# A decoder layer on one core: the gating unit between the last slabs of the input projection, and the first half of the output projection slab by slab between the heads of the attention

## The chip, the core and the metric

The kernel runs on one core of a Trainium2 chip. TensorE (PE) multiplies into PSUM, eight banks of 128 x 512 fp32; VectorE (DVE), ScalarE (ACT) and GpSimd (POOL) compute; SyncE (SP) starts most of the transfers between HBM and SBUF, POOL the others. The metric is the device time of one execution in microseconds (us). The median of three runs is 1489.71 us (1485.79 to 1490.67).

## The reference, cut to what matters

```python
mod = jnp.dot(jax.nn.silu(c), p['w_ada']) + p['b_ada']
shift1, scale1, gate1, shift2, scale2, gate2 = jnp.split(mod[:, None, :], 6, axis=-1)
h = x * (1 + scale1) + shift1
proj = jnp.dot(h, p['w_in'])
q, k, v, u_a, v_a = jnp.split(proj, [W_B, 2 * W_B, 3 * W_B, 3 * W_B + W_A], axis=-1)
...
attn = moba_attention(q, k_all, v_all, pos0, p['rel_bias'])
u_a = jax.nn.gelu(u_a)
v_a = layer_norm(jax.nn.gelu(v_a), p['ln_sgu_g'], p['ln_sgu_b'])
gm = chunk_spatial_gate(u_a, v_a, p['w_s'], p['b_s'])      # u_a * (w_s @ v_a + b_s)
mixed = jnp.concatenate([rms_norm(gm, p['norm_a_g']), rms_norm(attn, p['norm_b_g'])], axis=-1)
x = layer_norm(ALPHA * x + gate1 * jnp.dot(mixed, p['w_out']), p['ln1_g'], p['ln1_b'])
h = x * (1 + scale2) + shift2
up = jnp.dot(h, p['w_up'])                                  # then conv, silu, w_down, layer norm
```

There are 288 rows: 256 of one prompt and 32 of eight sampled sequences (four tokens each, with 256 old keys and values in pages of 128). The model width is 2048, with eight gating groups and eight attention heads of 128 columns. Everything is fp32.

## The kernel before

All activations lie transposed: a tile is 128 features by 288 rows. Each engine has one instruction stream, written out by hand, and semaphores join the streams; their order in the code is the order on the engine.

A weight matrix is read in **slabs** of 128 x 1024 fp32 (0.5 MB). ACT rounds a slab to fp32r (`hi`, tile wH), DVE subtracts to get the rest (`lo`, tile wL), and PE makes three products for each 128 x 128 block (L401 to L403), so 24 matmuls of 288 columns a slab (`products`). Four slabs are in flight (`RING`), three split ahead (`AHEAD`). ACT's `hi` for slab i+3 waits until slab i-1 is used. PE's `take` waits until the last reader of a PSUM bank has released it.

The **input projection** has 80 slabs: five chunks of the model width, ten groups of four output tiles in each; the last chunk is slabs 60 to 79, two for each group, and DVE adds each finished tile to `proj`. Between slabs stand **bursts** of four modulation slabs (`ada_slab`, w_ada, 0.5 MB each, ring of 8): 128 of the 192 modulation slabs are done there. When a unit of 16 is through, ACT copies it, PE turns it (`ada_turn`) and DVE adds it to modT (`mod_finish`).

After slab 79 comes everything that needs `proj`: transposes of v and of the gating unit's v_a, statistics, scaling, gate matmuls (wsT and bd), u times gate; then the attention in a loop over eight heads: scores of head h+1, the scores of one sampled sequence's old keys (`past_scores`, KV), one modulation slab, then softmax, transpose (`Pp` to `PTp`) and product with `Vrm`. Sixteen modulation slabs stand in the gating unit, eight between the heads, eight later. The **first half of the output projection** (slabs `S_OUT` to `S_OUT`+15, tiles 0 to 7 of the mixed rows, which come from the gating unit) starts after the last head, with the old values' products of the sampled sequences between the slabs; the **second half** (16 slabs, the attention's rows) follows, then a layer norm whose chain is DVE and ACT work (`normalise`, `centre`, `affine`), and the up projection.

KV is a double buffer of 1 MB halves; POOL refills a half (`load_kv`, two pages, two transfers) when the step that read it is through (`kv_used`).

Of the kernel before, what the change touches and what calls it, by code (L numbers as in the profile page):

```python
# [53 lines left out]
OUT_BANKS = (2, 3, 6, 7)  # L54
# [8 lines left out]
CHUNKS = [(0, 2), (2, 2), (4, 4), (8, 4), (12, 4)]  # L63
IN_SLABS = [(c, g, half) for c, (_, nk) in enumerate(CHUNKS) for g in range(IN_GROUPS) for half in range(nk // 2)]
# [9 lines left out]
def slab_columns(s):  # L74
# [7 lines left out]
TD_UP = [TD_OUT + 3 * n for n in (8, 20, 32)]  # L82
TD_DN = [TD_OUT + 3 * 16, TD_OUT + 3 * 28, TD_OUT + 3 * 37 + 1]
# [5 lines left out]
A_GATE, A_UP = 128, 160  # L89
# [19 lines left out]
def ada_turn_of(a):  # L109

    return a // ADA_RING if a < A_GATE else A_GATE // ADA_RING + (a - A_GATE) // RING


UNIT_END = {q: min(i for i in range(-1, IN_N) if ada_through(i) >= a + n) for q, (a, n, _, _) in enumerate(MOD_UNITS) if q}
# [4 lines left out]
V_ALL = V_CONV + 4 * 2 * FT  # L119
# [36 lines left out]
SBUF_BYTES = 212000  # L156
# [23 lines left out]
def decoder_layer_program(nc, io, n_phys):  # L180
    with ExitStack() as ctx:
# [42 lines left out]
        Vn, o_vn = place("Vn", [SAMP, 1024])  # L224
# [9 lines left out]
        VA, _ = place("VA", [P, 2 * 1024], over=o_va)  # L234
        Tm, _ = place("Tm", [P, 2 * 512], over=o_s4)
# [1513 lines left out]
```

## Time and profile before

| | |
|---|---|
| median of 3 runs | 1489.71 us |
| the profiled execution: its time, its span | 1491.05 us, 1489.3 us |
| PE busy over the span | 93% |
| DVE, ACT, POOL busy | 57%, 38%, 7% |
| end of the last input slab | about 343.5 us |
| first output slab starts | 442.06 us |
| second half of the output projection starts | 526.25 us |
| its last slab ends | 580.3 us |
| fifth slab of the up projection starts | 619.11 us |

The stretch rows below list for each stretch its length, then busy time with number of instructions for PE, PE's weight loads, DVE, ACT and POOL, then the mean granted TensorE clock (1.00 is 2.4 GHz, 0.5 is 1.2 GHz), the busy share of the DMA engines and GB/s. Timeline rows list start, duration, engine, line, operation, operands, count, and in brackets the idle time before and what ended it. An fp32 matmul counts as two records, a transpose or an fp32r one as one. Waiting rows list the total in us, the number of waits and the longest.

### The profile page before, as it was taken

What the parts mean: (1) busy time and instruction counts of PE and PEld (TensorE: products, weight loads), DVE (VectorE), ACT (ScalarE), POOL (GpSimd) and SP (SyncE); (2) the same over time, 40 slices, a digit from 0 to 9 for tenths busy, and PEclk for the clock granted to TensorE, in tenths of its full rate; (3) what the DMA queues carried; (4) which work ended last, traced back from release to release, by engine and by line L of the source; (5) the groups of instructions that cost most, each with busy time, mean ns of one, the idle gap of its engine ahead of it and who ended that gap; (6) DMA issues with size and microseconds to landing.
All of it is one profiled execution on the core that took longest, in us unless ns stands there. A gap on an engine that the chain in (4) does not pass through costs nothing.

```text
span 1489.3 us, 29006 instructions
## 1 busy us (share of the span) xinstructions
PE 1382.0 (93%) x11330; PEld 1298.3 (87%) x11330; DVE 851.8 (57%) x1353; ACT 569.1 (38%) x811; POOL 107.6 (7%) x249
## 2 busy tenths in 40 slices
PE   6999999996777997899999999999999999999992
PEld 4989898884446996789999999999999999999992
DVE  3486555546553566656566644557575545666555
ACT  3532222223241343734344333344444333444333
POOL 1000000003011000011011000001010000101001
PEclk9999999998799998899999999999999999999996
DMA  9999899988697444377645454454545454553621
GB/s 380 374 338 388 335 350 342 334 290 298 230 336 275 141 156 169 114 288 276 225 156 178 161 169 159 152 182 143 183 154 181 158 169 156 169 169 105 205 94 64
DMA packets 89806, 325.62 MB, mean 219 GB/s; under 512 B 10622, under 2 KB 10622, under 8 KB 89473
## 3 DMA queue, kind: packets, MB, share of 16 engines
q1 hardware_dynamic: 81792, 294.69, 56.2%
q0 software_dynamic: 6928, 24.87, 4.6%
q10 hardware_dynamic: 1008, 4.98, 0.8%
q8 instruction: 55, 0.90, 0.2%
q14 instruction: 23, 0.18, 0.0%
HBM read 318.83 MB, written 5.67 MB: 218 GB/s over the span
## 4 chain that ended last, share of the span: by engine, by line
PE 86%; DVE 4%; DMA 4%; ACT 3%; issue 1%; SPq 0%; POOLq 0%; ACTq 0%; POOL 0%; DVEq 0%
PE ps L401 26%; PE ps L403 25%; PE ps L402 25%; PE ps L417 5%; DMA KV<-values 1%; DMA ada<-w_ada 1%; DMA raw<-w_in 1%; ACT xT L955 1%; DVE wL L1062 1%; DMA KV<-keys 1%; PE ps L640 1%; PE ps L554 1%; DVE xT L1413 1%; DVE xT L1412 1%; PE ps L607 0%
## 5 line engine op out<-in xcount | busy, mean ns | idle before, releaser
L1062 DVE TENSOR_TENSOR wL<-raw,wH 128x1024 fp32r<-128x1024 f32 (+1 forms) x376 | 450.4, 1212 | 376.0 <-ACT wH L800 374.3
L800 ACT ACTIVATE wH<-raw 128x1024 fp32r<-128x1024 f32 (+1 forms) x376 | 392.1, 1050 | 639.4 <-PE ps L403 568.3
L401 PE MATMUL ps<-hL,wH 128*128 128x288 f32 x2016 | 603.2, 299 | 18.9 <-DVE hL L1434 8.3
L403 PE MATMUL ps<-hH,wH 128*128 128x288 f32 x2016 | 599.3, 297 | 0.0
L402 PE MATMUL ps<-hH,wL 128*128 128x288 f32 x2016 | 589.8, 293 | 0.0
L401 PEld LDWEIGHTS ps<-hL,wH 128*128 128x128 f32 x2016 | 380.6, 189 | 35.6 <-issue 21.6
L402 PEld LDWEIGHTS ps<-hH,wL 128*128 128x128 f32 x2016 | 385.8, 191 | 0.0
L403 PEld LDWEIGHTS ps<-hH,wH 128*128 128x128 f32 x2016 | 379.5, 188 | 0.0
L401 PE MATMUL ps<-ffL,wH 128*128 128x288 f32 x688 | 205.2, 298 | 2.8 <-ACT U L988 2.8
L402 PE MATMUL ps<-ffH,wL 128*128 128x288 f32 x688 | 203.6, 296 | 0.0
L403 PE MATMUL ps<-ffH,wH 128*128 128x288 f32 x688 | 203.1, 295 | 0.0
L1132 DVE TENSOR_TENSOR proj<-ps,proj 128x288 f32<-128x288 f32 x160 | 71.7, 457 | 117.6 <-PE ps L403 117.3
L401 PEld LDWEIGHTS ps<-ffL,wH 128*128 128x128 f32 x688 | 129.6, 188 | 4.0 <-issue 3.0
L403 PEld LDWEIGHTS ps<-ffH,wH 128*128 128x128 f32 x688 | 130.2, 189 | 0.0
L402 PEld LDWEIGHTS ps<-ffH,wL 128*128 128x128 f32 x688 | 129.8, 189 | 0.0
L401 PE MATMUL ps<-mix,wH 128*128 128x288 f32 x256 | 77.4, 303 | 0.3 <-DVE xT L1318 0.3
L402 PE MATMUL ps<-mix,wL 128*128 128x288 f32 x256 | 75.5, 295 | 0.0
L403 PE MATMUL ps<-mix,wH 128*128 128x288 f32 x256 | 75.3, 294 | 0.0
L417 PE MATMUL ps<-ada,cT 128*32 128x256 f32 x960 | 67.3, 407 | 6.7 <-DMA ada<-w_ada 6.7
L1627 POOL COPY E<-U 128x4 f32 (+1 forms) x44 | 11.2, 254 | 718.2 <-ACT U L988 718.2
L417 PEld LDWEIGHTS ps<-ada,cT 128*32 128x32 f32 x960 | 28.4, 114 | 28.0 <-DMA ada<-w_ada 9.2
L401 PEld LDWEIGHTS ps<-mix,wH 128*128 128x128 f32 x256 | 48.0, 187 | 4.0 <-issue 2.9
(212 smaller groups left out, 991.6 us busy)
## 6 DMA issues: line engine op xcount, KB each, us to landing
raw<-w_up SPq DMA_DIRECT2D x168, 512.0 KB, 3.5
ada<-w_ada SPq DMA_DIRECT2D x128, 512.0 KB, 6.5
raw<-w_down SPq DMA_DIRECT2D x84, 512.0 KB, 3.4
raw<-w_in SPq DMA_DIRECT2D x80, 512.0 KB, 8.3
adaX<-w_ada SPq DMA_DIRECT2D x32, 512.0 KB, 6.1
adaY<-w_ada SPq DMA_DIRECT2D x32, 512.0 KB, 7.8
raw<-w_out SPq DMA_DIRECT2D x32, 512.0 KB, 3.9
KV<-keys POOLq DMA_DIRECT2D x16, 512.0 KB, 5.8
```

Of the source, the lines that this page charges most:

```text
L401: nc.tensor.matmul(out, wH[:, w:w + P], rhs_lo(kk), start=start, stop=False)
L402: nc.tensor.matmul(out, wL[:, w:w + P], rhs_hi(kk), start=False, stop=False)
L403: mm = nc.tensor.matmul(out, wH[:, w:w + P], rhs_hi(kk), start=False, stop=stop)
L417: mm = nc.tensor.matmul(ps[32 * c:32 * c + 32, bank, 0:256], cT[:, 32 * k:32 * k + 32], src[:, 256 * c:256 * (c + 1)], start=(k == 0), sto ...
L554: mm = nc.tensor.matmul(b[:, 0:ROWS], ones[:, :], tile(proj, k0 + k), start=(k == 0), stop=(k == 7))
L640: mm = nc.tensor.transpose(b[0:n, t * P:(t + 1) * P], tile(S4, t, r * P, r * P + n), ident)
L800: nc.scalar.activation(wH[:, o:o + cols], raw[:, o:o + cols], ACT.Copy).then_inc(hi_done, 1)
L955: y = nc.scalar.activation(tile(xT, k), tile(xT, k), ACT.Identity, scale=vec[:, scale_at + k:scale_at + k + 1], bias=vec[:, bias_at + k:bi ...
L1062: vec_tt(wL[:, o:o + cols], raw[:, o:o + cols], wH[:, o:o + cols].bitcast(F32), ALU.subtract).then_inc(split_done, 1)
L1132: release(vec_tt(tile(proj, k), ps[:, k % 5, 0:ROWS], tile(proj, k), ALU.add), ("in", c, k))
L1412: steps.link(vec_tt(x, x, spread(RN[:, 0:1], [0, 4], [1, ROWS]), ALU.mult))
L1413: vec_tt(x, x, spread(RN[:, ROWS:ROWS + 1], [0, 4], [1, ROWS]), ALU.add).then_inc(xn_ready, 1)
```

## The change

The groups of the last chunk run in the order `LAST_ORDER`: v_a, u, v, q, k. The gating unit is spread over slabs 63 to 79: transposes of v_a and v, gate products and their DVE and ACT work stand between the slabs (`sgu_step`). The layer norm's scale and shift of v_a are no longer applied to v_a ahead of the gate product for the prompt: they enter through per-group columns in DVE's gate step (`gate`) and a row sum of w_s (`gate_rows`, two matmuls). For the sampled rows' output, POOL does the two remaining tensor operations on VAs (32 x 1024): the multiplication after the gate products, the addition after slab 79. The first half of the output projection is cut into slabs of four input tiles by two output tiles, so that it needs two PSUM banks and two slabs finish a pair of tiles; one such slab stands in each head's turn, the others between the old values' products. Its DVE steps (`accumulate_out`) come eight times, for two tiles each. Norm and square of the attention's rows are made for prompt and sampled rows apart. 112 modulation slabs stay in the input projection, 4 follow the last slab of the first half, 28 stand in bursts in the second half, 16 around the layer norm's PE work. ACT starts the norm of the gated rows (`root`) only after the store of VAs (`va_stored`), since its tile lies over VAs. The KV halves lie over hL and over adaY, so the second half is loaded after slab 79.

```diff
-OUT_BANKS = (2, 3, 6, 7)
+OUT_BANKS = (2, 3)
...
+LAST_ORDER = [8, 9, 6, 7, 4, 5, 0, 1, 2, 3]
...
-MOD_UNITS = [(0, HALF, 0, 16), (8, HALF, 2, 18), (16, 16, 4, 20), (32, 16, 8, 24), (48, 16, SH2, SH2 + 4), (64, 16, 12, 28),
-             (80, 16, SH2 + 8, SH2 + 12), (96, 16, SC2, SC2 + 4), (112, 16, SC2 + 8, SC2 + 12)]
-Q_GATE, Q_UP = 9, 11
+MOD_UNITS = [(0, HALF, 0, 16), (8, HALF, 2, 18), (16, 16, 4, 20), (32, 16, 8, 24), (48, 16, G1, G1 + 4), (64, 16, 12, 28),
+             (80, 16, G1 + 8, G1 + 12), (96, 16, SH2, SH2 + 4), (112, 16, SC2, SC2 + 4), (128, 16, SH2 + 8, SH2 + 12),
+             (144, 16, SC2 + 8, SC2 + 12)]
+GATE_UNITS = (4, 6)
...
-BURSTS = [2, 5, 8, 11, 14, 16] + [19 + 5 * k // 2 for k in range(24)]
+BURSTS = [2, 5, 8, 11, 14, 16] + [19 + 5 * k // 2 for k in range(20)] + [S_OUT + 15] + [S_OUT + 17 + 2 * k for k in range(7)]
...
+                if i == 63:
+                    turn_va(0, 0, 5)
...
+                if i == 72:
+                    gates(0, 0, 5)
+                    gates(0, 1, 7)
+                if i == 73:
+                    turn_v(0, 0, 6)
+                if i == 74:
+                    gates(1, 0, 6)
+                if i == 75:
+                    gates(1, 1, 5)
+                if i == 76:
+                    decode_gates(7)
+                    turn_v(1, 0, 6)
+                if i == 77:
+                    turn_v(2, 0, 5)
+                    turn_v(0, 1, 6)
+                if i == 78:
+                    turn_v(1, 1, 7)
...
+            def out_slab(n):
+                g, j = divmod(n, 2)
+                pe.wait_ge(m_split, 4 * j + 4)
+                products(S_OUT + n, n, lambda kk: mix_hi(4 * j + kk), lambda kk: mix_lo(4 * j + kk), OUT_BANKS, j == 0, j == 1, ktiles=4,
+                         taking=lambda t: take(pe, ("out a", g, t), OUT_BANKS[t]))
+                bursts_after(S_OUT + n)
...
+            scores(0)
+            take(pe, "S past 0", 6)
+            take(pe, "S past 1", 7)
+            past_scores(0)
+            new_scores()
+            for h in range(1, HEADS + 1):
+                if h < HEADS:
+                    scores(h)
+                if h >= 2:
+                    attend(h - 2)
+                if h < HEADS:
+                    past_scores(h)
+                out_slab(h - 1)
+                turn_probabilities(h - 1)
...
+            attend(HEADS - 1)
+            out_slab(8)
+            take(pe, "O 0", 0)
+            take(pe, "O 1", 1)
+            past_values(0)
+            sum_squares("sum b", 7, 2, 8, 0, SEQ)
+            past_values(1)
+            out_slab(9)
+            past_values(2)
+            out_slab(10)
+            past_values(3)
+            out_slab(11)
+            past_values(4)
+            past_values(5)
+            out_slab(12)
+            past_values(6)
+            past_values(7)
...
+            out_slab(13)
...
+            out_slab(14)
+            sum_squares("sum s", 4, 3, 8, SEQ, ROWS)
+            out_slab(15)
...
+                    bursts_after(S_OUT + 16 + 4 * g + j)
...
+            a = MOD_UNITS[U_SC2B][0]
+            for k in range(4):
+                ada_next(a + k)
             turn_rows(3, 0)
+            for k in range(4, 8):
+                ada_next(a + k)
             spread_rows(0)
+            for k in range(8, 16):
+                ada_next(a + k)
+            ada_turn(U_SC2B, ("turn", U_SC2B))
...
+                if issued <= A_LATE < limit:
+                    sp.wait_ge(kv_used, 2 * NSEQ)
...
+            def attention():
+                act.wait_ge(va_stored, 16)
+                act.wait_ge(v_stored, 16)
+                root(0, "sum a")
+                for k in range(4):
+                    mix_hi_at(k)
+                exponentials(0)
+                for k in range(4, 8):
+                    mix_hi_at(k)
+                act.wait_ge(k_stored, 16)
+                for h in range(1, HEADS + 1):
+                    if h >= 2:
+                        copy_turned(h - 2)
+                        out_step(h - 1)
+                        attended(h - 2)
+                    if h < HEADS:
+                        exponentials(h)
...
+            def gate(c, gg):
+                b = filled(dve, ("gate", c, gg))
+                released(dve, ("ws", gg))
+                for g in range(4 * gg, 4 * gg + 4):
+                    o = (g % 4) * P
+                    ins = vec_stt(b[:, o:o + P], b[:, o:o + P], vec[:, V_SG + g:V_SG + g + 1], BS[:, g * P:(g + 1) * P], ALU.mult, ALU.add)
+                steps.link(ins)
+                dve.wait_ge(gelu_ready, 3 + gg)
+                u = tiles(proj, 24 + 4 * gg, 4, c * P, (c + 1) * P)
+                release(vec_tt(u, u, b.rearrange("p (g t) -> p g t", g=4), ALU.mult), ("gate", c, gg))
+                if gg:
+                    released(dve, ("gate", c, 0))
+                    released(dve, ("gate", c, 1))
+                    dve.sem_inc(gm_ready, 1)
...
+            for h in range(1, HEADS):
+                logits(h)
+                probabilities(h - 1)
                 if h == 1:
-                    fold_norm()
-                if h == 2:
-                    invert_root(0)
-                    norm_rows(0, 0)
-                if h == 3:
-                    norm_rows(0, 1)
-                if h >= 5:
-                    mix_lo_at(2 * h - 10)
-                    mix_lo_at(2 * h - 9)
+                    for k in range(4, 8):
+                        mix_lo_at(k)
+                if h + 1 < NSEQ:
+                    own_queries(h + 1)
+                if h >= 2:
+                    out_step(h - 1)
+                if h % 2 == 0:
+                    accumulate_out(h // 2 - 1)
...
+            own_probabilities(1)
+            out_step(9)
+            own_probabilities(2)
+            own_probabilities(3)
+            invert_root(1, "sum b", 0, SEQ)
+            norm_rows(1, 0)
+            out_step(10)
+            accumulate_out(4)
+            own_probabilities(4)
+            norm_rows(1, 1)
+            out_step(11)
+            own_probabilities(5)
+            for k in range(8, 12):
+                mix_lo_at(k)
+            out_step(12)
+            accumulate_out(5)
...
+                if b4 == 1:
+                    unit_finish(U_SC2B)
...
+            in_done(pool, 8)
+            in_done(pool, 9)
+            pool.dma_start(io["kvT"][:, 0:8 * ROWS], proj[:, 8 * ROWS:16 * ROWS]).then_inc(k_stored, 16)
+            pool.wait_ge(used, IN_N)
             load_kv(1)
-            pool.wait_ge(va_ready, 3)
+            pool.wait_ge(vas_done, 1)
+            nc.gpsimd.tensor_tensor(VAs[:, :], VAs[:, :], SH[:, :], ALU.add).then_inc(vas_done, 1)
+            pool.wait_ge(vas_done, 2)
+            pool.dma_start(io["va"][:, :], VAs[:, :]).then_inc(va_stored, 16)
```

**PE, from the gating unit** (wsT, bd: gate weights; VA, VAs: scaled v_a; ada: modulation). Before, behind the input projection:

```order
L417 MATMUL ps<-ada,cT 32x256 x4
L507 MATMUL ps<-wsT,VA 128x128 x4
L417 MATMUL ps<-ada,cT 32x256 x8
L507 MATMUL ps<-wsT,VA 128x128 x4
L417 MATMUL ps<-ada,cT 32x256 x8
L507 MATMUL ps<-wsT,VA 128x128 x4
L417 MATMUL ps<-ada,cT 32x256 x8
L507 MATMUL ps<-wsT,VA 128x128 x4
L417 MATMUL ps<-ada,cT 32x256 x8
L514 MATMUL ps<-bd,VAs 128x32 x8
```

The changed kernel, from slab 72 on (L437 is the first matmul of an input slab):

```order
L527 MATMUL ps<-wsT,VA_82 128x128 x8
L437 MATMUL ps<-hL,wH 128x288
...
L519 MATMUL ps<-cst,proj 128x128 x4
L437 MATMUL ps<-hL,wH 128x288
...
L527 MATMUL ps<-wsT,VA_83 128x128 x4
L437 MATMUL ps<-hL,wH 128x288
...
L527 MATMUL ps<-wsT,VA_83 128x128 x4
L437 MATMUL ps<-hL,wH 128x288
...
L536 MATMUL ps<-bd,VAs 128x32 x8
L519 MATMUL ps<-cst,proj 128x128 x4
```

The gate products moved from between modulation slabs to between input slabs.

**PE, one head** (Qm, KV: old keys; Pp, PTp: probabilities; Vrm: values). Before:

```order
L535 MATMUL ps<-proj 128x128
L536 MATMUL ps<-proj 128x256
L544 MATMUL ps<-KV,Qm 32x256 x8
L417 MATMUL ps<-ada,cT 32x256 x4
L569 MATMUL ps<-cst,Pp 128x128 x3
L574 MATMUL ps<-PTp,Vrm 128x256
L575 MATMUL ps<-PTp,Vrm 128x128
```

The changed kernel, head 2's turn:

```order
L610 MATMUL ps<-proj 128x128
L611 MATMUL ps<-proj 128x256
L646 MATMUL ps<-PTp,Vrm 128x256
L647 MATMUL ps<-PTp,Vrm 128x128
L619 MATMUL ps<-KV_97,Qm 32x256 x8
L437 MATMUL ps<-mix,wH 128x288
...
L638 MATMUL ps<-cst,Pp 128x128 x3
```

The modulation slab is gone, an output slab (L437 with mix) stands ahead of the transpose, and the product with Vrm is that of the head before.

**DVE, between the old values' products** (wL: `lo` of a slab; PTm: masked probabilities; the rows with S and xT are `accumulate_out`). Before:

```order
L1062 TENSOR_TENSOR wL<-raw,wH 128x1024
L1332 TENSOR_TENSOR PTm<-PTs,cst 128x512
L1317 TENSOR_TENSOR S_68<-ps,modT 128x32
L1318 SCALAR_TENSOR_TENSOR xT<-ps,modT,xT 128x256
...
L1321 TENSOR_TENSOR xT<-xT,S_68 128x4x32
L1062 TENSOR_TENSOR wL<-raw,wH 128x1024
L1332 TENSOR_TENSOR PTm<-PTs,cst 128x512
```

The changed kernel, around output slab 13:

```order
L1260 TENSOR_TENSOR wL<-raw,wH 128x1024
L1614 COPY OS<-ps 128x128 x2
L1260 TENSOR_TENSOR wL<-raw,wH 128x1024
L1525 TENSOR_TENSOR S_68<-ps,modT 128x32
L1526 SCALAR_TENSOR_TENSOR xT<-ps,modT,xT 128x256
L1525 TENSOR_TENSOR S_68<-ps,modT 128x32
L1526 SCALAR_TENSOR_TENSOR xT<-ps,modT,xT 128x256
L1529 TENSOR_TENSOR xT<-xT,S_68 128x2x32
L1260 TENSOR_TENSOR wL<-raw,wH 128x1024
```

In both a `lo` stands next to `accumulate_out`; in the changed kernel it is ahead of each pair of tiles, and the slab that PE starts next after a pair needs the same two banks.

## Rows read from the trace of the kernel before

**Rows 1.** Busy time by stretch, all engines; each stretch: length, then each engine.

```profile
...
60.00:343.50 283.50, 283.35 (x2590) 253.41 (x2582) 165.47 (x274) 81.95 (x88) 2.16 (x4) 1.00 0.91 339
343.50:442.00 98.50, 67.49 (x537) 40.30 (x538) 56.67 (x128) 34.36 (x71) 22.36 (x40) 0.83 0.81 287
442.00:526.20 84.20, 73.19 (x761) 66.56 (x759) 40.95 (x74) 26.52 (x35) 9.90 (x18) 0.96 0.59 212
526.20:580.30 54.10, 54.05 (x408) 53.49 (x408) 34.01 (x63) 19.08 (x18) 0.00 (x0) 1.00 0.56 185
580.30:619.10 38.80, 21.85 (x153) 19.72 (x152) 26.66 (x45) 27.53 (x44) 0.00 (x0) 0.78 0.15 55
...
```

**Rows 2.** What PE waited for, 343.5 to 442 us.

```profile
...
PE ps L417 <- DMA ada<-w_ada: 6.7, 3, 4.4
PE ps L574 <- ACT PTp L891: 6.1, 8, 1.4
...
```

**Rows 3.** The same, 442 to 526 us.

```profile
...
PE ps L607 <- DMA KV<-values: 7.3, 2, 6.1
...
```

**Rows 4.** Timeline of PE, the gating unit and one head of attention.

```profile
...
282.82 1.93 PE L417 MATMUL ps<-ada,cT 128*32 128x256 f32 x32
...
345.05 2.84 PE L489 MATMUL ps<-cst,proj 128*128 128x128 f32 x24 [1.71 <-DVE small L1154]
...
376.17 1.16 PE L507 MATMUL ps<-wsT,VA 128*128 128x128 f32 x8
...
383.72 3.62 PE L514 MATMUL ps<-bd,VAs 32*128 32x32 f32 x16
...
401.39 4.12 PE L554 MATMUL ps<-proj,ones 128*128 128x288 f32 x16
...
410.35 1.07 PE L544 MATMUL ps<-KV,Qm 128*32 128x256 f32 x16
...
413.72 0.67 PE L574 MATMUL ps<-PTp,Vrm 128*128 128x256 f32 x2 [0.67 <-ACT PTp L891]
414.23 0.38 PE L575 MATMUL ps<-PTp,Vrm 128*128 128x128 f32 x2
...
```

**Rows 5.** Timeline of PE, one slab between two steps of the old values.

```profile
...
470.53 1.08 PE L607 MATMUL ps<-KV,PTm 128*32 128x128 f32 x32
...
471.98 0.40 PE L401 MATMUL ps<-mix,wH 128*128 128x288 f32 x1
...
475.36 0.86 PE L607 MATMUL ps<-KV,PTm 128*32 128x128 f32 x24
```

**Rows 6.** Transfers issued from 343 to 530 us: size, median us to landing.

```profile
...
KV<-values POOLq DMA_DIRECT2D x16, 512.0 KB, 6.4
...
va<-VAs POOLq DMA_DIRECT2D x1, 128.0 KB, 9.0
```

**Rows 7.** Timeline of POOL: the second page of a load.

```profile
...
473.97 0.53 POOL L1584 DMA_DIRECT2D KV<-values  x1 [0.61 <-issue]
```

**Rows 8.** Timelines of DVE and ACT: parts of the norm, a table load.

```profile
...
406.92 1.95 DVE L1246 RECIPROCAL RR<-RR 128x288 f32<-128x288 f32 x1
...
395.60 1.28 ACT L883 ACT_TABLE_LOAD   x1 [4.84 <-DVE small L1269]
...
419.79 0.95 ACT L874 ACTIVATE mix<-proj,vec 128x288 fp32r<-128x288 f32 x2
...
```

**Rows 9.** Timelines of POOL and DVE at the end of the program.

```profile
...
1468.58 3.75 POOL L1649 TENSOR_TENSOR xT<-xT,RN 128x1152 f32<-128x1152 f32 x1 [84.77 <-DVE RN L1406]
...
1468.51 1.36 DVE L1412 TENSOR_TENSOR xT<-xT,RN 128x1152 f32<-128x1152 f32 x1
1469.90 3.65 DVE L1413 TENSOR_TENSOR xT<-xT,RN 128x1152 f32<-128x1152 f32 x1
...
```

**Rows 10.** Timeline of DVE, the second low part of the normalised rows.

```profile
...
602.89 1.36 DVE L1434 TENSOR_TENSOR hL<-H,hH 128x1152 fp32r<-128x1152 f32 x1 [0.50 <-ACT hH L972]
```

More of the change, by code:

```diff
@@ L151, in shape_constants @@
     return c, hot
[L156 removed]
+SBUF_BYTES = 212800
 class Steps:
@@ L474, in _ @@
                     fill(nc.tensor.matmul(b[0:HEADS, 0:REL_N], rbias[:, :], hot[:, :], start=True, stop=True), "bias")
-            def ada_slabs(unit, first, last):
-                for k in range(first, last):
-                    a = A_GATE + ADA_STEPS * (unit - 4) + k
-                    ada_slab(a % RING, ada_turn_of(a), k, unit - 4 + Q_GATE, 6 if unit == 4 else 5)
-            pe.wait_ge(proj_ready, 1)
-            for hg in range(2):
-                for r in range(3):
-                    job, n = ("v", r, hg), P if r < 2 else SAMP
-                    b = take(pe, job, 3 * hg + r)
-                    for h in range(4):
-                        mm = nc.tensor.transpose(b[0:n, h * P:(h + 1) * P], tile(proj, 16 + 4 * hg + h, r * P, r * P + n), ident)
-                    fill(mm, job)
@@ L621, in _ @@
             fill(mm, "O 1")
-            ada_turn(Q_GATE + 1, ("turn", "gate", 1), bank=4)
-            out_slabs(9, 11)
+            out_slab(13)
             released(pe, "O 0")
@@ new lines, in gate_bias, with va_statistics @@
+            def gate_bias(half):
+                dve.wait_ge(sgu_in, 16 * 3)
+                b = filled(dve, ("ws", half))
+                for g in range(4 * half, 4 * half + 4):
+                    row = BS[:, g * P:(g + 1) * P]
+                    ins = vec_stt(row, b[:, (g % 4) * P:(g % 4 + 1) * P], vec[:, V_SB + g:V_SB + g + 1], row, ALU.mult, ALU.add)
+                release(ins, ("ws", half))
+            def va_statistics(r, hg):
+                n = P if r < 2 else SAMP
+                released(dve, ("va", r, hg))
+                return nc.vector.bn_stats(small[0:n, 12 * r + 6 * hg:12 * r + 6 * hg + 6], (VA0, VA1, VAs)[r][:, hg * 512:(hg + 1) * 512])
@@ new lines, in gate_decode @@
+            def gate_decode():
+                b = filled(dve, "gate decode")
+                for g in range(HEADS):
+                    o = b[:, g * SAMP:(g + 1) * SAMP].rearrange("p (n t) -> p n t", t=TOK)
+                    ins = vec_stt(o, o, vec[:, V_SG + g:V_SG + g + 1], spread(BS[:, g * P:g * P + 1], [0, NSEQ], [1, TOK]), ALU.mult, ALU.add)
+                steps.link(ins)
+                u = tiles(proj, 24, 8, SEQ, ROWS)
+                release(vec_tt(u, u, b[:, 0:256].rearrange("p (g t) -> p g t", g=HEADS), ALU.mult), "gate decode")
+                released(dve, "gate decode")
+                dve.sem_inc(gm_ready, 1)
@@ L1143, in _ @@
                     _, n, first, second = MOD_UNITS[q]
-                    mod_finish(("turn", q), (first, second), n=2 if n == HALF else 4)
+                    mod_finish(("turn", q), (first, second), gate=q in GATE_UNITS, n=2 if n == HALF else 4)
                     if q == 2:
@@ L1325, in _ @@
+            out_step(7)
+            dve.wait_ge(s_exp, 1)
+            steps.link(nc.vector.reciprocal(small[:, 60:62], small[:, 60:62]))
+            for hh in range(2):
+                ins = vec_ts(Ls[:, hh * ROWS:(hh + 1) * ROWS], Ls[:, hh * ROWS:(hh + 1) * ROWS], small[:, 60 + hh:61 + hh], None, ALU.mult)
+            ins.then_inc(s_prob, 1)
+            accumulate_out(3)
+            out_step(8)
             b = filled(dve, "s PN")
```

820 lines of the change are left out of this document (454 added, 366 removed).

## The prediction

> **What bounds the kernel now.** First the busy time by stretch [rows 1]. In the input projection PE is busy 283.35 of 283.50 us, DVE 165.47 (58%), while the DMA engines move 339 GB/s: PE bounds it, and transfers at that rate do not hold it up. Then come 98.5 us, the gating unit and the heads, with 67.49 us of PE work at a mean clock of 0.83; then 84.2 us with PE at 73.19, the first half of the output projection with the old values; then 54.1 us of second half, all PE; then 38.8 us of layer norm, where PE has 21.85. So 31.0 and 11.0 us of PE's time are empty in the second and third stretch, and none of PE's own slabs stand in the second to cover its waits. Second, the waits there [rows 2]: 6.7 us for late modulation slabs, 6.1 in eight waits for ACT's copy of the turned probabilities; in the third [rows 3] 7.3 us for old values. The changed kernel moves PE work into these holes. What counts is therefore PE's instructions, one by one, plus the waits that stay.
>
> **Prices.** Sixteen slabs and three row turns fill 54.1 us [rows 1], so a slab is about 3.25 us; alone between other work 3.35 (from 471.98 to 475.36, [rows 5]). From [rows 4]: four modulation slabs 1.87 us; a transpose 2.84 / 24 = 0.12; a gate job of four matmuls 1.1; the eight decode gates 1.8 if the 3.62 us was at half clock, as I take it, 3.6 if not; sum of squares 4.0 (8 matmuls of 288 columns), so 0.9 for one of 512 columns and 3.6 for eight of 256; old scores 1.0; product with Vrm 0.9. Old values 1.0 [rows 5]. Scores of a head have the columns of a Vrm product, 0.8.
>
> **A, input projection: +6.6 us.** Removed: 16 modulation slabs, 7.4, and one turn, 0.2. Added on PE: 44 transposes 5.2, gates 4.4, decode gates 1.8, two row sums 1.8. That is +5.6. DVE gains some 11,000 columns at 1.18 ns (1.36 / 1152, [rows 9]) and 50 instructions at about 0.1, so 18 us, most of it in 20 slabs or 75 us; it has 42% free, and ACT is emptier still [rows 1]. The chain gelu, copy, statistics, root, scale has at least one slab between any two steps; only the first gelu is close: after slab 62 ACT has a `hi`, a table load of 1.28 [rows 8] and the gelu, with about 1 us for each of the two passes 3.3 us, against one slab. I add 1 us of waits.
>
> POOL's multiplication falls between these slabs. At the end of the program a POOL operation on 1152 columns took 3.75 us, and the DVE tensor_tensor that ran beside it took 3.65 us instead of 1.36 [rows 9]. So DVE may be held 2.3 us once here, which a slab of lead covers. The Trainium skill (SBUF — State Buffer, Who interferes with whom) says that a DVE instruction with two SBUF inputs contends with a GpSimd instruction that reads SBUF, and that the loser blocks for the whole instruction; the trace agrees (3.65 against 1.36), and by the rule too the sum stays, unless DVE is already late, which is a rival below.
>
> **B, from the last input slab to the second half: 128 us instead of 98.5 + 84.2 = 182.7, so -54.7.** Time from the end of slab 79:
>
> - Prelude, 18.5. POOL issues the K store and two pages of the second KV half (3.4 at 1.13 apart), then adds on 1024 columns (3.75 x 1024 / 1152 = 3.3 [rows 9]), then issues the store of VAs, at 7. That store landed after 9.0 us before [rows 6], behind a transfer of 688 KB; here most of what is ahead has had 5 us, so I take 4 (bounds 2 and 9). ACT waits for it. Then table load 1.3, root 0.5, reciprocal 1.95, normalising 1.4 (as a 1152-column operation in [rows 9]), four high parts 1.9 [rows 8], last low part 0.5. PE has about 8.5 us of work meanwhile; the rest is a hole, and it makes the clock fall: +2 in all, counted at the end.
> - Heads, 49.8. Head 1: slab 3.35, turn 0.4, wait 0.4. Six heads of scores 0.8, Vrm 0.9, old scores 1.0, slab 3.35, turn 0.4 = 6.4, and 0.3 of waits. One first wait of 0.8. The last 4.7. The slab covers softmax and ACT's copy, so the 6.1 us of [rows 2] go. DVE has 2,750 columns and 14 instructions in each, by the count above 4.7 us, ACT fewer; both are less than PE's.
> - Sampled probabilities, last Vrm product, slab 8: 5.8 with 0.5 of wait.
> - Old values, 36. A half comes back 8.8 us after the step that frees it: the second page is issued 2.4 us after that step ([rows 5]: ends at 471.6; [rows 7]: 473.97) and lands 6.4 later [rows 6]. Step 1 ends 5.9 after step 0 starts (sum of squares between), and steps 3, 5, 7 hang on each other: 5.9 + 3 x 9.9 = 35.6. PE's work in it is 25, so 11 us are waits, more than the 7.3 of [rows 3].
> - Rest, 16: new values 0.5, slab 13, transposes 0.5, 2.4 of waiting for two banks (`hi`, then `lo`, then the first `accumulate_out` step, 2.9 us behind slab 13), slab 14, 0.4, slab 15, four modulation slabs 1.9. The norm of the sampled rows is ready by then.
> - Clock 2. Sum 18.5 + 49.8 + 5.8 + 36 + 16 + 2 = 128.
>
> **C, second half: +15.1.** Seven bursts 13.1, two turns 0.5, and 1.5 for loads that come late. It moves 28 + 16 slabs of 0.524 MB in 68 us, 339 GB/s, the rate at which PE did not wait before [rows 1].
>
> **D, layer norm: +0.9.** Its end is set by ACT and DVE; 16 modulation slabs (7.5 us) lie in PE's 17 us of idle time [rows 1]. ACT gains one copy (0.4), DVE about 1.5 us of which 0.5 was a wait [rows 10].
>
> The modulation slabs are 192 in both; nothing else changes. Sum: 6.6 - 54.7 + 15.1 + 0.9 = -32.1. The profiled execution took 1491.05, so 1459.0; it lies 1.3 above the median of 1489.71, so **1458**.
>
> **The rivals.** What a measurement of this kernel can tell from no change is about 0.3%, 4.5 us.
>
> 1. As forecast, 1444 to 1471: 0.60. The bounds are the VAs store (-2, +5), the old values (a landing of 9.0 like that of the store would give 3 x 2.6 = +8, no waits at all -11), decode gates (+1.8), the clock (-2, +3), heads without their 0.3 (-2).
> 2. DVE is late in the last 20 slabs, so the gating unit is not hidden: 0.12. For it: `gate` and adds share the stream, and POOL holds DVE. Against: 42% free. If half its 18 us shows, 1467; all of it, 1476.
> 3. Loads: 0.11. Bursts each second slab in C, where the input projection has them each two to three slabs; each late by 1 us gives +7, with +8 for values 1473.
> 4. Slabs between heads don't do what they are there for: 0.05. If each head keeps the 0.8 us that it waited for ACT (6.1 / 8, [rows 2]), +6: 1464.
> 5. Quicker: 0.09. If the store lands in 2 us and value halves in time, 1440.
> 6. Slower than before: 0.03. The gate is in the layer norm: ACT copies the last modulation unit ahead of the second block (about 19 us behind the last output slab: that block's low part starts 22.6 behind it [rows 10], 2.1 of products and 1.2 of `hi` after the copy), and hH's upper half lies over the ring. The 16 loads at 339 GB/s take 25 us and one landing 6, so even all of them issued late cost 12 us (1470). Only above 19 + 32 = 51 us, 3.2 us a slab, it decides. Against: half of them are issued before the last slab ends.
>
> Outside 1442 to 1473 I leave 0.2: half of the quicker case, part of 2 and 3. All cases but the last, and a remainder of 0.01, are faster by over 0.3%: faster 0.96, same 0.01, slower 0.03.
>
> **What would show it.** In the profile after: the last input slab ends near 350; PE waits there under 2 us. The first output slab starts 18 to 19 us later, and the root ahead of it waits for the store of VAs. Each head repeats after 6.7 us with no wait over 1. PE's largest wait is for the values, 9 to 11 us in the steps 2 to 7. The second half has seven bursts without a wait and takes 69 us. The fifth slab of the up projection starts at 587. The prediction is wrong if DVE's adds hold PE's banks in slabs 72 to 79, if heads take over 8 us, or if the bursts of the second half wait for w_ada.

## The result, and the profile after

The changed kernel takes 1484.95 us (median of 10 runs, 1480.1 to 1489.0), the kernel before in the same session 1489.35 us (10 runs, 1485.79 to 1495.2). The ratio is 0.997, with a 95% interval from 0.9958 to 0.9983. So it is faster by about 0.3%, where 2% was forecast.

The stretches of PE in the profiled execution after (span 1486.6 us): cut at the end of the last input slab, the start of the second half of the output projection, the end of its last slab, the start of the fifth slab of the up projection, the end. The columns are those of [rows 1].

```profile
60.00:352.00 292.00, 290.56 (x2575) 262.96 (x2568) 182.67 (x327) 100.21 (x111) 16.69 (x26) 1.00 0.86 316
352.00:482.70 130.70, 106.88 (x980) 91.07 (x977) 74.74 (x165) 46.31 (x102) 20.59 (x39) 0.90 0.61 218
482.70:552.70 70.00, 70.00 (x656) 62.07 (x656) 34.42 (x69) 19.85 (x20) 0.00 (x0) 1.00 0.90 337
552.70:607.20 54.50, 30.54 (x283) 23.70 (x282) 27.41 (x50) 27.66 (x45) 0.00 (x0) 0.78 0.47 174
607.20:1486.60 879.40, 845.29 (x6384) 833.64 (x6384) 507.57 (x738) 349.83 (x502) 69.06 (x175) 0.98 0.50 169
```

One cut of [rows 1] is not at that event. Sixteen slabs of 24 matmuls are 384, 128 for each of the three products. Between 526.2 and 580.3 the kernel before has 124 of each; after, between 482.7 and 552.7, it is 128:

```profile
L402 PE MATMUL ps<-mix,wL 128*128 128x288 f32 x124 | 36.6, 295 | 0.0
```

```profile
L438 PE MATMUL ps<-mix,wL 128*128 128x288 f32 x128 | 37.7, 295 | 0.0
```

In the kernel before the second half starts at 524.24. What starts at 526.25 is its 13th matmul, the first that needs a bank of the first half:

```profile
526.25 0.40 PE L401 MATMUL ps<-mix,wH 128*128 128x288 f32 x1 [0.26 <-DVE xT L1318]
```

So B was 180.8 us long and C 56.1; the table has it so.

Where the time went, in us:

| stretch | before | after | difference | forecast |
|---|---|---|---|---|
| to the end of the last input slab (A) | 343.4 | 352.0 | +8.6 | +6.6 |
| to the second half (B) | 180.8 | 130.7 | -50.1 | -54.7 |
| second half (C) | 56.1 | 70.0 | +13.9 | +15.1 |
| to the fifth up slab (D) | 38.8 | 54.5 | **+15.7** | +0.9 |
| from there to the end | 870.2 | 879.4 | **+9.2** | 0 |
| sum (spans) | 1489.3 | 1486.6 | -2.7 | -32.1 |

The parts on which the prediction spent its work (A, B, C) are each off by 1 to 5 us; the large loss is in two places that it took for settled. The waits of PE after, first from slab 79's end to the second half, then from the second half to the fifth up slab (total, number, longest):

```profile
PE ps L619 <- DMA KV<-keys: 6.8, 1, 6.8
PE ps L667 <- DMA KV<-values: 6.0, 3, 3.7
PE ps L437 <- DVE mix L1486: 4.8, 1, 4.8
PE ps L437 <- DVE xT L1526: 4.8, 2, 2.8
PE ps L646 <- ACT PTp L1030: 0.7, 1, 0.7
```

```profile
PE ps L749 <- DVE DG L1663: 17.4, 1, 17.4
PE ps L494 <- ACT adaS L920: 4.0, 1, 4.0
PE ps L437 <- DVE wL L1260: 2.5, 1, 2.5
```

The same stretch of the kernel before:

```profile
PE ps L401 <- DVE hL L1434: 8.3, 1, 8.3
PE ps L650 <- DVE DG L1401: 4.1, 1, 4.1
PE ps L401 <- DVE wL L1062: 3.0, 1, 3.0
PE ps L640 <- DVE S L1378: 1.6, 1, 1.6
```

DG is the diagonal matrix of the layer norm's root, the end of its chain of statistics. PE's products with it start 22.6 us after the last slab's end (575.32 - 552.72), before 7.2 us after it (587.46 - 580.30): 15.4 us later, nearly all of the 15.7 us that D lost. The timeline shows why that chain is late. ACT, then SP's queue, then DVE, each from PE's last slab (552.7) on:

```profile
568.49 1.06 ACT L908 ACTIVATE wH<-raw 128x1024 fp32r<-128x1024 f32 x1 [18.04 <-DMA raw<-w_up]
569.46 1.15 ACT L1133 ACTIVATE xT<-S 128x1152 f32<-128x1152 f32 x1
```

```profile
553.34 1.75 SPq L843 DMA_DIRECT2D ada<-w_ada  x4
556.67 0.91 SPq L843 DMA_DIRECT2D adaX<-w_ada  x2
557.62 1.22 SPq L843 DMA_DIRECT2D adaY<-w_ada  x2
559.20 0.35 SPq L835 DMA_DIRECT2D raw<-w_up  x1
```

```profile
569.58 1.23 DVE L1260 TENSOR_TENSOR wL<-raw,wH 128x1024 fp32r<-128x1024 f32 x1 [15.51 <-ACT wH L908]
570.72 1.88 DVE L1646 BATCH_NORM_STATS2 small<-ps 128x6 f32<-128x512 f32 x3
...
574.11 1.16 DVE L1663 TENSOR_SCALAR DG<-cst,small 128x128 f32<-128x128 f32 x6
```

Read it from below. DVE's statistics (L1646) need nothing but what PE had ready, but on DVE they stand behind the low part of the fourth up slab, which waits for ACT's high part. ACT's high part stands ahead of its copy for the residual (L1133) and waits 18.04 us for the transfer of that slab. SP issued this transfer at 559.20, because it stands behind eight w_ada transfers. Each of them waits until PE has read the modulation slab that was in its ring slot, and these are the first eight of the sixteen that now stand around the layer norm (PE reads four at 552.64, the next four from 555.97 to 557.9). The w_up transfer then took 9.3 us to land. Nothing in the layer norm needs the slab; it only stands in front.

The last stretch, 9.2 us longer, has the same 6384 PE instructions as before. PE is busy 845.29 us there; over the same stretch of the kernel before (619.1 to 1489.3) the windows gave:

```profile
619.10:1489.30 870.20, 836.73 (x6384) 825.27 (x6384) 506.62 (x738) 349.96 (x502) 68.45 (x175) 0.98 0.51 171
```

So the matmuls themselves became slower: the middle one of the three up projections, in which PE never waits, has 1536 of them in both kernels, and the starts of its products hH times wL run from 930.1 to 1132.8 before (202.7 us) and from 920.0 to 1126.1 after (206.1 us). Grouped by operands, the three products of the input and up projection over the whole kernel (busy us, mean ns), before and then after:

```profile
L401 PE MATMUL ps<-hL,wH 128*128 128x288 f32 x2016 | 603.2, 299 | 18.9 <-DVE hL L1434 8.3 <-DVE wL L1062 5.4 <-DVE hL L1100 4.7
L403 PE MATMUL ps<-hH,wH 128*128 128x288 f32 x2016 | 599.3, 297 | 0.0
L402 PE MATMUL ps<-hH,wL 128*128 128x288 f32 x2016 | 589.8, 293 | 0.0
```

```profile
L437 PE MATMUL ps<-hL,wH 128*128 128x288 f32 x2016 | 604.0, 300 | 9.3 <-DVE wL L1260 4.8
L438 PE MATMUL ps<-hH,wL 128*128 128x288 f32 x2016 | 602.1, 299 | 0.0
L439 PE MATMUL ps<-hH,wH 128*128 128x288 f32 x2016 | 601.0, 298 | 0.0
```

By duration one of the three changed: hH times wL, from 293 to 299 ns, 12.3 us in 2016 matmuls. (Records overlap and their ends are modelled, so the time between starts, used further on, says more.) The change does nothing to these tiles, except in one way: `vec` has 16 more columns, and every tile placed behind it, wH and wL among them, lies 64 bytes higher. hH and hL stand ahead of `vec` and did not move.

### The profile page after: what moved, and what is told of

It is laid out like the page before. It is cut to its first block, busy times and chain, and to the rows that moved or that the text cites. A ratio compares the mean times of both kernels' runs of the same rounds, so it can differ in the third digit from the quotient of the medians.

```text
span 1486.6 us, 29173 instructions
## 1 busy us (share of the span) xinstructions
PE 1389.8 (93%) x11350; PEld 1314.0 (88%) x11350; DVE 847.9 (57%) x1379; ACT 572.9 (39%) x832; POOL 111.1 (7%) x252
## 4 chain that ended last, share of the span: by engine, by line
PE 89%; DVE 4%; DMA 3%; ACT 2%; issue 1%; SPq 0%; POOL 0%; POOLq 0%; ACTq 0%; DVEq 0%
PE ps L437 27%; PE ps L438 26%; PE ps L439 26%; PE ps L453 5%; ACT xT L1150 1%; DMA adaY<-w_ada 1%; DMA KV<-values 1%; PE ps L739 1%; DVE wL L1260 1%; DMA raw<-w_up 1%; DVE xT L1675 1%; DVE xT L1674 1%; DMA raw<-w_down 1%; ACT H L1164 1%; PE ps L749 0%
## 5 line engine op out<-in xcount | busy, mean ns | idle before, releaser
L437 PE MATMUL ps<-hL,wH 128*128 128x288 f32 x2016 | 604.0, 300 | 9.3 <-DVE wL L1260 4.8
L438 PE MATMUL ps<-hH,wL 128*128 128x288 f32 x2016 | 602.1, 299 | 0.0
L437 PEld LDWEIGHTS ps<-hL,wH 128*128 128x128 f32 x2016 | 382.2, 190 | 23.1 <-issue 11.2
L438 PEld LDWEIGHTS ps<-hH,wL 128*128 128x128 f32 x2016 | 381.3, 189 | 0.5 <-issue 0.5
L437 PE MATMUL ps<-ffL,wH 128*128 128x288 f32 x688 | 205.8, 299 | 3.6 <-ACT U L1185 3.6
L437 PEld LDWEIGHTS ps<-ffL,wH 128*128 128x128 f32 x688 | 130.1, 189 | 5.0 <-issue 4.0
L439 PEld LDWEIGHTS ps<-ffH,wH 128*128 128x128 f32 x688 | 130.7, 190 | 0.0
L437 PE MATMUL ps<-mix,wH 128*128 128x288 f32 x256 | 81.4, 318 | 9.6 <-DVE mix L1486 4.8
L439 PE MATMUL ps<-mix,wH 128*128 128x288 f32 x256 | 78.1, 305 | 0.0
L437 PEld LDWEIGHTS ps<-mix,wH 128*128 128x128 f32 x256 | 51.0, 199 | 16.5 <-issue 10.7
L453 PE MATMUL ps<-ada,cT 128*32 128x256 f32 x832 | 51.7, 390 | 0.0
L438 PEld LDWEIGHTS ps<-mix,wL 128*128 128x128 f32 x256 | 51.1, 200 | 0.0
```

The source lines that it names most:

```text
L437: nc.tensor.matmul(out, wH[:, w:w + P], rhs_lo(kk), start=start, stop=False)
L438: nc.tensor.matmul(out, wL[:, w:w + P], rhs_hi(kk), start=False, stop=False)
L439: mm = nc.tensor.matmul(out, wH[:, w:w + P], rhs_hi(kk), start=False, stop=stop)
L453: mm = nc.tensor.matmul(ps[32 * c:32 * c + 32, bank, 0:256], cT[:, 32 * k:32 * k + 32], src[:, 256 * c:256 * (c + 1)], start=(k == 0), sto ...
```

## The experiments

Two theories for D: Q, the queue position of the w_up transfer; and a rival P, the modulation slabs in the layer norm by their own PE work and copy (near the prediction's rival 6). Two for the last stretch: A, the addresses; and a rival, something the change does to transfers or to the clock. The first four runs share a chip and 11 runs of the kernel before (1488.34 us); the changed kernel was measured in another session, beside 1489.35 us, so differences to it hold to about 1 to 2 us.

**e1: the fourth w_up slab is issued ahead.**

```diff
-                elif s < S_UP[0] + AHEAD:
+                elif s < S_UP[0] + AHEAD + 1:
...
-            stream(S_UP[0] + 35, io["w_up"], 35, 29)
+            stream(S_UP[0] + 36, io["w_up"], 36, 28)
```

> The changed kernel with one transfer earlier: the load of the up projection's fourth slab is issued ahead of the last twelve modulation loads instead of behind them, and the following ones keep their order. Theory Q (the layer norm is held because ACT's hi for that slab stands ahead of ACT's part of the norm, and its data is queued behind modulation loads that wait for PE): PE's 17.4 us wait for DG falls to about 2 to 4, and the time falls by 14 to 16 us, to about 1470. Rival P (the sixteen modulation slabs around the norm hold it by their own PE work and copy): under 3 us.

Measured: 1465.49 us (1462.4 to 1468.91), ratio 0.9853 [0.9832, 0.9875], 19.5 below the median of after. ACT now takes the slab 2.35 us after the one before, and it no longer waits for a transfer:

```profile
548.82 1.06 ACT L908 ACTIVATE wH<-raw 128x1024 fp32r<-128x1024 f32 x1 [2.35 <-PE ps L439]
550.10 1.17 ACT L1133 ACTIVATE xT<-S 128x1152 f32<-128x1152 f32 x1 [0.23 <-DVE S L1640]
```

PE's wait for DG falls from 17.4 to 1.9 us, and its products with DG start 7.1 us after the last slab's end (555.81 - 548.72), as in the kernel before. D falls from 54.5 to 37.5 us. The modulation slabs and the gate are still in the layer norm, so rival P can hold little of the loss. The median fell by 2.5 us more than D. Of that, about 1 us is the difference between the sessions. And the middle up projection runs faster here (its starts of hH times wL span 204.4 us, after 206.1) though no tile has moved: the same addresses gave two paces, and why is open.

**e2: the kernel before, with an unused tile of 64 bytes behind `vec`.**

```diff
         vec, _ = place("vec", [P, V_ALL])
+        gap, _ = place("gap", [P, 16])
```

> The kernel before with nothing changed but an unused gap of 64 bytes a partition behind vec, so that cst, raw, wH, wL, proj, ffH and ffL lie 64 bytes higher, as they do in the changed kernel. Theory A (the place of the operands in SBUF sets a matmul's pace): four slabs of the up projection take 13.1 us instead of 12.95, and the time rises by 6 to 9 us. Rival N (the pace differs for another reason, chip or run): within 2 us of the kernel before.

Measured: 1498.14 us (1495.37 to 1501.1), ratio 1.0066 [1.0046, 1.0086]. A tile that nobody reads costs 9.8 us. The product hH times wL takes 299 ns here too, and in the middle up projection its starts span 206.1 us, as after. The addresses are a cause by themselves.

**e3: the changed kernel, with the 16 columns in a tile of their own at the end,** so that everything else lies where it did before.

```diff
-        vec, _ = place("vec", [P, V_ALL])
+        vec, _ = place("vec", [P, V_SG])
...
+        sgc, _ = place("sgc", [P, 2 * HEADS])
```

> The changed kernel with the sixteen new columns of vec in a tile of their own at the end, loaded by a transfer of their own, so that raw, wH, wL, proj and all behind them lie at the addresses of before. Theory A: 6 to 9 us faster than the changed kernel, about 1477, four slabs at 12.95 us. Rival N: as the changed kernel, within 2 us.

Measured: 1473.33 us (1472.33 to 1476.93), ratio 0.9899 [0.9881, 0.9918], 11.6 below after. The last input slab ends at 348.71 instead of 351.84, so up to 3.1 of the 8.6 us of A were the address as well (2.6 in e2 against before; e1, with the addresses of after, ended it at 350.88).

**e4: e1 and e3 together.**

> Both edits of the two runs before on the changed kernel. Theories Q and A together: 22 to 25 us faster than the changed kernel, about 1461, which is the forecast within its own error. If only Q holds 1470, if only A 1477.

Measured: 1456.95 us (1454.08 to 1462.85), ratio 0.9791 [0.9767, 0.9816]; 28.0 below after, against 19.5 + 11.6 = 31.1 for the two apart. By the ratios to the kernel before, which leave the sessions out, it is 26.7 against 17.4 + 10.6 = 28.0. With both losses gone the kernel takes about what the prediction had said, 1458; how far that is luck stands below.

What is left to ask is the prelude, which the prediction put down to the store of VAs, and the transfers. Three runs that build on e4, and one on the addresses, share a chip and 9 runs of before (1488.11 us).

**e5: the root's tile `RR` in the second half of `S4`, not over VAs.**

```diff
-        RR, _ = place("RR", [P, 2 * ROWS], over=o_vas)
+        RR, _ = place("RR", [P, 2 * ROWS], over=o_s4 + 8 * ROWS)
...
-                act.wait_ge(va_stored, 16)
+                act.wait_ge(vas_done, 1)
```

> e4 with the tile of the root (RR) in the second half of S4 instead of over VAs, so that ACT waits for POOL's multiplication of VAs and not for the store. In e4 ACT's root started at 362.18, after 12.27 us of waiting for that store, and the first output slab at 368.59 after a wait of 5.5 us. Theory S (the store sets the prelude, as the forecast's B has it): the first output slab follows the product of the second sequence's old keys directly, 4 to 5 us earlier, about 1452. Rival K (the keys' landing sets it, or the recovered time is given back at the keys' wait): under 1.5 us gained, 1456.

Measured: 1452.05 us (1448.28 to 1453.03), ratio 0.975 [0.9733, 0.9768], 4.9 below e4. ACT's root in e4 and then in e5:

```profile
362.18 0.50 ACT L1010 ACTIVATE RR<-ps,small 128x288 f32<-128x288 f32 x1 [12.27 <-DMA va<-VAs]
```

```profile
353.18 0.50 ACT L1010 ACTIVATE RR<-ps,small 128x288 f32<-128x288 f32 x1 [3.28 <-PE ps L546]
```

PE's wait for mix (5.5 us) is gone and the first output slab starts at 363.06 instead of 368.59, directly behind the old keys' product. Theory S held. What bounds the prelude now is the wait for the keys, 5.5 us.

**e6: the second half of the keys ahead of the store of K in POOL's queue.**

```diff
-            pool.dma_start(io["kvT"][:, 0:8 * ROWS], proj[:, 8 * ROWS:16 * ROWS]).then_inc(k_stored, 16)
             pool.wait_ge(used, IN_N)
             load_kv(1)
+            pool.dma_start(io["kvT"][:, 0:8 * ROWS], proj[:, 8 * ROWS:16 * ROWS]).then_inc(k_stored, 16)
```

> e5 with POOL's two transfers of the second half of the keys ahead of the store of K (1.15 MB) instead of behind it. In e4 they were issued at 351.1 and 353.0 and PE waited 5.4 us for them until 361.1. Theory Q (the transfers stand behind the store in POOL's queue): PE's wait for keys falls by 2 to 4 us and the time by as much against e5. Rival L (the landing takes 6.4 us whatever is ahead, and slab 79's end gates the issue at 350.5): under 1 us gained, since only the issue of one store (0.6 us) goes.

Measured: 1448.17 us (1446.96 to 1449.64), ratio 0.973 [0.9715, 0.9745], 3.9 below e5, with intervals and runs that overlap. The time would suit theory Q, the trace does not. PE's wait for the keys only fell from 5.5 to 4.9:

```profile
353.77 1.07 PE L620 MATMUL ps<-KV,Qm 128*32 128x256 f32 x16
360.71 1.86 PE L620 MATMUL ps<-KV,Qm 128*32 128x256 f32 x16 [4.90 <-DMA KV<-keys]
```

The transfers were issued at 351.16 and 352.33, instead of 351.07 and 352.96: slab 79's end gates them whatever stands ahead (the rival L). The fifth up slab starts at 578.32 against 578.79 in e5, so most of the 3.9 us lies behind it, in stretches that the edit doesn't touch; from there to the end the profiled executions took 869.7 and 872.5 (868.6 in e4). That is the last down projection and the wait ahead of it: its products took 76.3 us in e3 and e5 and 74.8 in e4, e6 and e7, with the same code. So it varies from one execution to the next, and the queue's order is not shown to be worth more than half a microsecond.

**e7: `accumulate_out` ahead of the next slab's low part, for the last four pairs of tiles.**

```diff
-            out_step(12)
             accumulate_out(5)
+            out_step(12)
```

(and likewise for pairs 4, 6 and 7)

> e6 with DVE's accumulate_out ahead of the low part of the next slab (out_step) for the last four pairs of tiles. PE waits in e4 for xT (the release of banks 2 and 3) twice, 4.7 us in all. If the order on DVE makes these waits (the low part waits for ACT's high part, 1.1 us, which starts with the same slab's end), they fall to about 1 us and the time falls by 3 to 4 us against e6. If the waits only move to the low part of a slab (weights late), under 1 us.

Measured: 1444.33 us (1443.19 to 1445.3), ratio 0.9707 [0.9692, 0.9722], 3.8 below e6. PE's waits from slab 79's end to the second half, in e7:

```profile
PE ps L668 <- DMA KV<-values: 6.8, 3, 4.6
PE ps L620 <- DMA KV<-keys: 5.0, 2, 4.8
PE ps L647 <- ACT PTp L1031: 0.7, 1, 0.7
PE ps L692 <- ACT PTp L1031: 0.7, 1, 0.7
```

The two waits for xT (4.6 us in e6) are gone and the second half starts at 466.1 instead of 470.2 in e6 (482.7 in after), with runs that all lie below those of e6. Only transfers of keys and values are left of any size.

**e8: the kernel before, with the 64-byte tile `cw` ahead of `wH`.** Now only wH, wL and the tiles behind them up to `small` move.

```diff
+        cw, _ = place("cw", [P, 16])
         wH, _ = place("wH", [P, RING * SLAB], F32R)
...
-        cw, _ = place("cw", [P, 16])
```

> before with the 64-byte tile cw placed ahead of wH instead of behind small: wH, wL, ada, adaS, past, wsT, bd and small lie 64 bytes higher, all else where it was. Theory W (the place of PE's weights costs the time that e2 lost): +7 to +10 us, 1496 to 1499, matmuls in the input projection 1337 ps apart. Theory M (it is the place of something else: raw, cst, the moving tiles ffH and ffL of the down projection): within 2 us of before in the input and up stages, where hH and hL have not moved in e2 either, so that raw would be left.

Measured: 1495.01 us (1493.98 to 1496.47), ratio 1.005 [1.0036, 1.0064], +6.9 us. The same product is the slow one:

```profile
L402 PE MATMUL ps<-hH,wL 128*128 128x288 f32 x2016 | 600.3, 298 | 0.0
```

Theory W held for the input and up projections. In the input projection all products together start 133.8 ns apart on average, against 132.4 before (the expectation's 1337 ps is to be read as 133.7 ns). The intervals of e2 and e8 overlap, but the traces tell them apart: the down projection became faster here. The middle one, before and then e8, by the first and last start:

```profile
L402 PE MATMUL ps<-ffH,wL x256: 290/295/298, 1133.2 to 1235.8; 128*128 128x288 f32 x128
```

```profile
L402 PE MATMUL ps<-ffH,wL x256: 292/295/298, 1135.8 to 1237.6; 128*128 128x288 f32 x128
```

That is 102.6 us before and 101.8 in e8; in e2, where ffH and ffL moved with the weights, it is as before (1136.3 to 1238.8). Over the three down projections the 0.7 us make about 2.

Three more on the addresses, with 29 runs of before (1488.55 us).

**e9: `cw` and `pages`, 64 bytes each, ahead of `wH`:** the weights move by 128 bytes.

> before with the tiles cw and pages, 64 bytes each, placed ahead of wH instead of behind small: wH, wL, ada and the others up to small lie 128 bytes higher. e8, with 64 bytes, took 1495.01 us against 1488.11. Theory P (what counts is the place within 128 bytes): as before, 1486 to 1490, matmuls of the input projection 1323 ps apart. Rival D (the distance to something else counts, or every new place costs): 1493 or more, 1337 ps apart.

Measured: 1488.91 us (12 runs, 1485.97 to 1491.36), ratio 0.9998 [0.9985, 1.0011]. No loss, and the product is back at 293 ns:

```profile
L402 PE MATMUL ps<-hH,wL 128*128 128x288 f32 x2016 | 590.6, 293 | 0.0
```

Theory P of this run held for these two shifts: 64 bytes cost, 128 don't.

**e10: an unused tile of 32 bytes ahead of `wH`** (all behind it moves).

> before with an unused tile of 32 bytes ahead of wH: wH, wL and all tiles placed behind them lie 32 bytes higher. This is a scan, no theory gives a number. If the loss of e8 grows with the distance, half of it: 1491 to 1492. If it depends on a boundary of 64 bytes, either nothing or the whole: 1488 or 1495 to 1498.

Measured: 1489.74 us (12 runs, 1487.37 to 1493.44), ratio 1.0003 [0.9991, 1.0014]. No loss either, though hH times wL is not at its best here (296 ns); hL times wH fell from 299 to 297 instead, and the middle up projection takes as long as before (202.7 us by the same starts).

**e11: an unused tile of 64 bytes ahead of the region** that holds proj and later ffH and ffL.

> before with an unused tile of 64 bytes ahead of the region (proj, Vrm, Vn, VAs, and later ffH, ffL, U, CV, SA): only these lie 64 bytes higher. e2 moved everything and lost 9.8 us, e8 the weights alone and lost 6.9. Theory R (PE's moving operands ffH and ffL carry the rest): +2 to +4 us, 1490 to 1492, lost in the down projection. Rival (raw, cst or nothing carries it): within 1 us of before.

Measured: 1486.17 us (12 runs, 1482.78 to 1488.69), ratio 0.9975 [0.9964, 0.9987]. Theory R fell: this shift gains, 2.4 us by the medians. The trace shows where: the middle down projection takes 101.8 us by its starts, as in e8, where it was the weights that moved by 64 bytes.

```profile
L403 PE MATMUL ps<-ffH,wL x256: 289/295/296, 1132.3 to 1234.1; 128*128 128x288 f32 x128
```

**e12: e7 with e11's tile.**

> e7 with an unused tile of 64 bytes ahead of the region (proj, Vrm, later ffH, ffL). In before this edit took 1486.17 against 1488.55 us, ratio 0.9975 with an interval from 0.9964 to 0.9987. If that gain is one of the place of these tiles it adds to e7's: 1441 to 1443 us, ratio to before 0.967 to 0.970. If it was chance, e7's time again: 1444 to 1445, ratio 0.9707.

Measured: 1444.22 us (5 runs, 1441.03 to 1445.23), ratio 0.9695 [0.9679, 0.971]. Against e7's 0.9707 [0.9692, 0.9722] the times tell nothing apart: inconclusive. In the traces the gain is there, and hidden by other spread: the middle down projection takes 101.8 us against 102.6 in e7, and from the fifth up slab to the end it is 866.8 against 868.8, but the stretch B is 2.5 us longer than in e7. e7 and e12, 2.9 to 3.1% under before, are the fastest versions here.

## Why the prediction was wrong, step by step

**What bounded the kernel** was read rightly: PE's time and its holes between the last input slab and the up projection. B, the part of it up to the second half, shrank by 50.1 us. The price of a slab was read from a wrong count: the 54.1 us hold 15.5 slabs and three turns, not 16. With sixteen it is 56.1. So a slab takes 3.2 us and not 3.25, and the cut made B of the kernel before 2 us too long, so the sum -32.1 should have been about -30, and the forecast 1460.

**A (+6.6, measured +8.6).** The gating unit is hidden: PE waits 1.4 us between 60 and 352, and DVE's adds are never late, so rival 2 did not come. With the address mended (e4) A is 5.4, one below the term.

**B (128, measured 130.7).** The mechanism was right; its sizes were off both ways. The prelude took 20.5 (372.36 - 351.84) instead of 18.5: the store of VAs was issued 7.7 us in, forecast 7, though POOL's addition took 2.38 against 3.3, and landed 6.4 us later where 4 was taken. And the wait for the second half of the keys (6.8) was not seen as a term at all; it lay beside the wait for the store and set the prelude only in e5. A head repeats after 6.3 us, forecast 6.7. The old values took 36.4 us, forecast 36, with 6.0 us of waits for the values instead of 11, and one of 2.0 for xT, which e7 took away. The hold of DVE by POOL came as forecast, once and without effect: while POOL's addition ran, an operation on 64 columns took 1.23 us, and 0.22 right after it.

```profile
356.87 2.38 POOL L1886 TENSOR_TENSOR VAs<-VAs,SH 32x1024 f32<-32x1024 f32 x1
```

```profile
358.11 1.23 DVE L1537 TENSOR_TENSOR SBi<-E,cst 128x64 f32<-128x64 f32 x1
359.72 0.22 DVE L1540 TENSOR_TENSOR SBi<-SBi,cst 128x64 f32<-128x64 f32 x1
```

This is what the Trainium skill (SBUF — State Buffer, Who interferes with whom) describes, a DVE instruction with two SBUF inputs blocked beside a GpSimd one that reads SBUF; the trace agrees (1.23 us, ended 0.09 us after POOL's).

**C (+15.1, measured +13.9).** Seven bursts, no wait of PE, 337 GB/s; the 1.5 us for late loads were not needed. Rival 3 did not come.

**D (+0.9, measured +15.7): the step that failed.** The prediction wrote "Its end is set by ACT and DVE; 16 modulation slabs (7.5 us) lie in PE's 17 us of idle time". That counted the moved slabs as PE work. That part held: in e1, with the slabs in place, D takes 37.5 us against 38.8 before. It didn't count them as transfers on SP's queue, with the one w_up transfer behind them that ACT waits for ahead of the chain: 18.0 us on ACT, 17.4 on PE. Rival 6 came near. It put the layer norm's loss at up to 12 us, with a chance of 0.03, but it asked when the modulation data arrives, not what else is late behind it. e1 shows the cause: one load issued earlier, with everything else left in place, takes the wait for DG from 17.4 to 1.9 us.

**"Nothing else changes" (0, measured +9.2, and up to 3 more in A).** The diff showed V_ALL growing by 16 columns, and `place` sets one tile after the other. The prediction did not look at this, and no rival covered it. e2 and e8 show the cause in the kernel before alone; e3 takes it away from the changed one.

Without the two losses (e4, profiled execution) the stretches are, against the kernel before: A +5.4, B -48.8, C +14.0, D -1.3, the rest -1.7, together -32.4. With B of the kernel before cut rightly the forecast's terms are +6.6, -52.8, +15.1, +0.9 and 0, together -30.2. That the sum of e4 meets the recorded -32.1 is in part luck: B is 4.0 us worse than forecast, the others are together 6.2 better, and the slip of 2 us closes the gap. B alone also varies by 4 us between profiled executions in which its code is the same (127.8 in e1, 132.0 in e4). The range from 1442 to 1473 had room for the sizes of B, and none for a mechanism outside the list.

## What to carry to other kernels

When work is moved, follow its transfers through the issuing queue, and ask for the first instruction behind them what stands behind it in turn on the engine that consumes it: here a transfer that nobody needed yet held ACT, DVE and then PE for 17 us. When a tile grows, the others behind it move, and a change of addresses alone can be worth half a per cent; put new small tiles at the end, or compare with the kernel before plus a gap, before the difference is put down to the edit.

## What the runs showed of the hardware

The pace of fp32r matmuls with 128 x 288 operands depends on where the tiles lie in SBUF. With wH and wL 64 bytes higher the kernel took 6.9 us more; at 128 bytes higher nothing was lost, nor at 32 in sum. With only the region (proj and mix, later ffH and ffL) 64 bytes higher it took 2.4 us less.

Put in order by one number, these runs agree with each other. It is the distance from the moving tile (hH and hL, or ffH and ffL) to the weight tile, modulo 128 bytes, worked out from the sizes that `place` is given; it is the same for both tiles of a pair and for wH and wL. The table has the mean time between one matmul's start and the next, in ns (gaps of 0.2 us and more left out), in the middle up projection (hH, hL) and the middle down projection (ffH, ffL), where PE never waits:

| distance mod 128 | runs | hi, wH | hi, wL | lo, wH | all |
|---|---|---|---|---|---|
| 0 | ff in before, after, e2, e9, e10 | 132.9 to 133.2 | 133.4 to 133.9 | 133.1 to 133.3 | 133.3 |
| 32 | h in before, e3, e9, e11 | 133.1 | 129.0 | 134.6 to 134.7 | 132.2 |
| 64 | h in e10 | 132.5 | 132.5 | 131.7 | 132.2 |
| 64 | ff in e8, e11 | 132.4, 132.5 | 132.5 | 131.7 | 132.2 |
| 96 | h in e1, e8 | 134.9, 134.2 | 133.0, 132.8 | 132.1, 133.0 | 133.3 |
| 96 | h in after, e2 | 135.4 | 135.8 | 132.1 | 134.4 |

Two different pairs of tiles have the same three paces at 64. The products with mix in the second half fit as well: 133.2 to 133.4 ns at 0 and 132.5 at 64 (e8, e11). The change took hH and hL from 32 to 96; ffH and ffL, which moved along with the weights, stayed at 0. This is an order found in the traces behind the runs: no run was planned for it, only these four distances occur, and at 96 there are two paces that the distance does not tell apart. The mechanism stays open.
